# Forgetting attention with its query blocks in the order last, third, first, second, two of them in one group

## The reference

```
proj = hn @ fox_w_in[j]
qc, kc, vc, fz = split(proj)
log_f = log_sigmoid(fz + fox_b_f[j])
c = cumsum(log_f)                                   # per head, over the tokens
# per block of 128 queries:
logits = (q_block @ k^T) * HEAD_DIM ** -0.5 + c[query] - c[key]
logits = where(key <= query, logits, -inf)
out    = softmax(logits) @ v
mixed  = out @ fox_w_out[j]
```

## Time and profile before

| | |
|---|---|
| median of 3 runs | 2126.46 us (2125.49 to 2126.67) |
| span of the profiled execution | 2125.2 us |
| mean granted TensorE clock | 0.998 |
| TensorE busy | 2088.4 us (98%) |
| VectorE, ScalarE, GpSimd busy | 1435.0, 852.2, 748.9 us |
| the forgetting attention's iterations 1 to 8 | from about 1470 to 1669 us of the span |

### The profile page before, as it was taken

One profiled execution on the slowest core, in us unless ns is written; L12 is line 12 of the kernel. 1 busy time (PEld: TensorE's weight loads), 2 busy tenths in 40 slices (PEclk: granted clock), 3 DMA queues, 4 the chain that ended last, 5 costly groups with the idle time before them and its releaser, 6 DMA issues.

```text
span 2125.2 us, 37888 instructions
## 1 busy us (share of the span) xinstructions
PE 2088.4 (98%) x15232; PEld 1808.2 (85%) x15232; DVE 1435.0 (68%) x1748; ACT 852.2 (40%) x1154; POOL 748.9 (35%) x646
## 2 busy tenths in 40 slices
PE   8999999999989999999999999999999999999998
PEld 6989898778887899999788898987776689998977
DVE  7847576679757866666778575766666677575774
ACT  6434243454233433333444243434444344343434
POOL 2333244546433214243443151433333322423343
PEclk9999999999999999999999999999999999999999
DMA  5333332321012334243342332424223232433332
GB/s 160 90 109 103 97 86 85 97 60 41 14 33 61 101 91 119 79 117 88 100 123 77 107 105 86 119 70 120 79 79 95 74 99 80 120 90 106 89 93 90
DMA packets 366507, 192.95 MB, mean 91 GB/s; under 512 B 11038, under 2 KB 363408, under 8 KB 366368
## 3 DMA queue, kind: packets, MB, share of 16 engines
q1 hardware_dynamic: 364128, 185.11, 31.0%
q0 software_dynamic: 2224, 5.86, 0.9%
q10 hardware_dynamic: 16, 0.00, 0.0%
HBM read 188.81 MB, written 2.13 MB: 90 GB/s over the span
## 4 chain that ended last, share of the span: by engine, by line
PE 89%; DVE 7%; ACT 2%; issue 1%; DMA 0%; ACTq 0%; POOL 0%; DVEq 0%; SPq 0%; POOLq 0%
PE bank L468 13%; PE bank L470 13%; PE bank L469 13%; PE bank L633 11%; PE bank L634 11%; PE bank L635 11%; PE bank L1914 3%; PE bank L2575 2%; DVE w_lo L458 2%; PE bank L2577 2%; PE bank L2576 2%; PE bank L1255 1%; PE bank L1257 1%; PE bank L1256 1%; PE bank L2592 1%
## 5 line engine op out<-in xcount | busy, mean ns | idle before, releaser
L458 DVE TENSOR_TENSOR w_lo<-w_raw,w_hi 128x2048 fp32r<-128x2048 f32 (+3 forms) x192 | 393.4, 2049 | 137.6 <-ACT w_hi L453 136.6
L453 ACT CAST w_hi<-w_raw 128x2048 fp32r<-128x2048 f32 (+3 forms) x192 | 281.6, 1467 | 387.2 <-PE bank L635 169.7
L619 POOL TENSOR_TENSOR sums<-w_raw 128x512 f32<-128x512 f32 x68 | 95.8, 1409 | 778.0 <-DMA w_raw<-in_ffn_w_gu_dram 520.4
L468 PE MATMUL bank<-h_hi,w_hi 128*128 128x512 f32 x704 | 275.4, 391 | 1.8 <-DVE w_lo L458 1.5
L469 PE MATMUL bank<-h_hi,w_lo 128*128 128x512 f32 x704 | 274.2, 389 | 0.0
L470 PE MATMUL bank<-h_lo,w_hi 128*128 128x512 f32 x704 | 274.1, 389 | 0.0
L975 DVE SCALAR_TENSOR_TENSOR x<-bank,x 128x512 f32<-128x512 f32 (+1 forms) x96 | 66.4, 691 | 166.5 <-PE bank L470 165.5
L468 PEld LDWEIGHTS bank<-h_hi,w_hi 128*128 128x128 f32 x704 | 132.1, 188 | 34.8 <-issue 4.8
L633 PE MATMUL bank<-t_hi,s_hi 128*128 128x256 f32 x544 | 154.4, 284 | 1.7 <-issue 1.7
L470 PEld LDWEIGHTS bank<-h_lo,w_hi 128*128 128x128 f32 x704 | 132.1, 188 | 27.6
L469 PEld LDWEIGHTS bank<-h_hi,w_lo 128*128 128x128 f32 x704 | 132.2, 188 | 26.2
(11 more groups left out here) (390 smaller groups left out, 5444.5 us busy)
## 6 DMA issues: line engine op xcount, KB each, us to landing
w_raw<-in_ffn_w_gu_dram SPq DMA_DIRECT2D x176, 512.0 KB, 5.0
w_raw<-in_ffn_w_down_dram SPq DMA_DIRECT2D x128, 256.0 KB, 3.1
w_raw<-in_ffn_w_down_dram SPq DMA_DIRECT2D x64, 192.0 KB, 3.1
w_raw<-in_even_w_in_dram SPq DMA_DIRECT2D x40, 256.0 KB, 3.2
w_raw<-in_ple_w_gate_dram SPq DMA_DIRECT2D x16, 512.0 KB, 3.7
w_raw<-in_fox_w_in_dram SPq DMA_DIRECT2D x16, 512.0 KB, 5.0
w_raw<-in_even_w_out_dram SPq DMA_DIRECT2D x16, 256.0 KB, 3.4
w_raw<-in_fox_w_in_dram SPq DMA_DIRECT2D x16, 256.0 KB, 4.1
```

Source lines behind the costliest of these rows:

```text
L453: nc.scalar.copy(w_hi[slot][:, 0:tiles], w_raw[slot][:, 0:tiles]).then_inc(w_hi_ready, 1)
L458: nc.vector.tensor_tensor(w_lo[slot][:, 0:tiles], w_raw[slot][:, 0:tiles], w_hi[slot][:, 0:tiles].bitcast(F32), ALU.subtract).then_inc(w_r ...
L468: nc.tensor.matmul(dst, w[0], hi[:, k], start=k == 0, stop=False)
L619: nc.gpsimd.tensor_tensor(sums[:, 0:4], w[:, 8:12], w[:, 12:16], ALU.add).then_inc(sums_made, 1)
```

## The change

The units of a pair come in another order of query blocks, and two of them are handled together on TensorE. `FOX_ORDER = (3, 2, 0, 1)`: unit 0 is still the last block (512 columns) and unit 1 the third (384), but unit 2 is now the first block (128 columns) and unit 3 the second (256). 384 and 128 columns fill one bank of 512, so unit 2 is placed from column 384 on (`unit_place`) in the same banks as unit 1, for the products as for the transposes.

`logits(1, 2)` makes the products of both units one behind the other after a single wait, and signals `qk_done` once, by 2, at the end. `transposes(1, 2)` does the same for the transposes. `transposes` signals `pt_ready` in every case only once, at its end, where it signalled behind each head before. There is thus one run of weight groups fewer to interrupt: the products come ahead of weight groups 0, 5 and 9 (before: 0, 5, 8 and 10), the transposes ahead of groups 12, 16 and 20 (before: 12, 15, 18 and 21). The orders of the other engines stay as they were, unit by unit; only the block that a unit stands for and its columns in the bank differ.

The core of the diff:

```
+FOX_ORDER = (3, 2, 0, 1)
...
-            qb = NB - 1 - u
+            qb = FOX_ORDER[u]
             return qb * (qb + 1) // 2 * P, (qb + 1) * P
+
+        def unit_place(u):
+
+            return (NB - 1) * P if u == 2 else 0
...
-                def logits(u):
+                def logits(*units):
                     if not attend:
                         return
-                    if u == 0:
+                    if units[0] == 0:
                         pe.wait_ge(banks_free, n - 1)
                         pe.wait_ge(logit_ready, a * (2 * NB)) if not isinstance(a, int) or a else None
                     else:
-                        pe.wait_ge(logit_ready, a * (2 * NB) + 2 * u)
...
+                        pe.wait_ge(logit_ready, a * (2 * NB) + 2 * units[0])
+                    for u in units:
+                        qb = FOX_ORDER[u]
+                        for h in range(2):
+                            rows = slice(h * HD, (h + 1) * HD)
+                            mm = nc.tensor.matmul(bank[4 + h][:, unit_place(u):unit_place(u) + (qb + 1) * P],
+                                                  fox_q[rows, qb * P:(qb + 1) * P],
+                                                  fox_k[rows, 0:(qb + 1) * P], start=True, stop=True)
+                    mm.then_inc(qk_done, len(units))
...
+                def transposes(*units):
...
-                    for h in range(2):
-                        pe.wait_ge(p_ready, a * (2 * NB) + (2 * u + h + 1))
-                        for kb in range(qb + 1):
-                            mm = nc.tensor.transpose(bank[6 + h][:, kb * P:(kb + 1) * P],
-                                                     fox_logit[:, h, at + kb * P:at + (kb + 1) * P],
-                                                     ident[:])
-                        mm.then_inc(pt_ready, 1)
+                        pe.wait_ge(pt_copied, a * (2 * NB) + 2 * units[0])
+                    for u in units:
+                        qb = FOX_ORDER[u]
+                        at, _ = unit_cols(u)
+                        for h in range(2):
+                            pe.wait_ge(p_ready, a * (2 * NB) + (2 * u + h + 1))
+                            for kb in range(qb + 1):
+                                to = unit_place(u) + kb * P
+                                mm = nc.tensor.transpose(bank[6 + h][:, to:to + P],
+                                                         fox_logit[:, h, at + kb * P:at + (kb + 1) * P],
+                                                         ident[:])
+                    mm.then_inc(pt_ready, 2 * len(units))
...
-                logits(1)
-                groups(5, 8)
-                logits(2)
-                groups(8, 10)
+                logits(1, 2)
+                groups(5, 9)
                 logits(3)
-                groups(10, 12)
+                groups(9, 12)
                 transposes(0)
-                groups(12, 15)
-                transposes(1)
-                groups(15, 18)
-                transposes(2)
-                groups(18, 21)
+                groups(12, 16)
+                transposes(1, 2)
+                groups(16, 20)
                 transposes(3)
-                groups(21, 24)
+                groups(20, 24)
```

More of the change, by code:

```diff
@@ L2587, in logits @@
                     else:
-                        pe.wait_ge(logit_ready, a * (2 * NB) + 2 * u)
-                    qb = NB - 1 - u
-                    for h in range(2):
[L2591 to L2597, removed]
+                        pe.wait_ge(logit_ready, a * (2 * NB) + 2 * units[0])
[8 more added lines that the diff above has]
+                def transposes(*units):
                     if not attend:
                         return
-                    qb = NB - 1 - u
-                    at, _ = unit_cols(u)
-                    if u == 0:
+                    if units[0] == 0:
                         pe.wait_ge(vt_copied, a + 1)
@@ L2606, in transposes @@
                     else:
-                        pe.wait_ge(pt_copied, a * (2 * NB) + 2 * u)
-                    for h in range(2):
-                        pe.wait_ge(p_ready, a * (2 * NB) + (2 * u + h + 1))
-                        for kb in range(qb + 1):
-                            mm = nc.tensor.transpose(bank[6 + h][:, kb * P:(kb + 1) * P],
-                                                     fox_logit[:, h, at + kb * P:at + (kb + 1) * P],
-                                                     ident[:])
-                        mm.then_inc(pt_ready, 1)
+                        pe.wait_ge(pt_copied, a * (2 * NB) + 2 * units[0])
[10 more added lines that the diff above has]
+                    mm.then_inc(pt_ready, 2 * len(units))
                 def times_values():
@@ L2725, in copy_pt @@
                         nc.scalar.copy(fox_pt[:, h, 0:qb + 1, qb * P:(qb + 1) * P],
-                                       bank[6 + h][:, 0:(qb + 1) * P].rearrange("p (k q) -> p k q", q=P)
+                                       bank[6 + h][:, unit_place(u):unit_place(u) + (qb + 1) * P].rearrange("p (k q) -> p k q", q=P)
                                        ).then_inc(pt_copied, 1)
@@ L2802, in logits @@
                         return
-                    qb = NB - 1 - u
+                    qb = FOX_ORDER[u]
                     at, cols = unit_cols(u)
+                    place = unit_place(u)
                     dve.wait_ge(qk_done, a * NB + (u + 1))
@@ L2811, in logits @@
                             nc.vector.scalar_tensor_tensor(
-                                fox_logit[:, h, at:at + qb * P], bank[4 + h][:, 0:qb * P], cq[h],
+                                fox_logit[:, h, at:at + qb * P], bank[4 + h][:, place:place + qb * P], cq[h],
                                 fox_c[:, h, 0:qb * P], ALU.add, ALU.subtract)
                         nc.vector.scalar_tensor_tensor(
-                            fox_logit[:, h, at + qb * P:at + cols], bank[4 + h][:, qb * P:cols], cq[h],
+                            fox_logit[:, h, at + qb * P:at + cols], bank[4 + h][:, place + qb * P:place + cols], cq[h],
                             fox_cm[:, h, qb], ALU.add, ALU.subtract).then_inc(logit_ready, 1)
@@ L2898, in pair @@
                             fox_logit[:, h, at:at + cols], fox_logit[:, h, at:at + cols],
-                            fox_rcp[:, NB - 1 - u, h:h + 1].broadcast_to([P, cols]), ALU.mult
+                            fox_rcp[:, FOX_ORDER[u], h:h + 1].broadcast_to([P, cols]), ALU.mult
                         ).then_inc(p_ready, 1)
```

## The result

The changed kernel takes 2132.81 us (median of 8 runs, 2132.15 to 2135.31), the kernel before 2126.43 beside it: a ratio of 1.0029 with a 95% interval of 1.0021 to 1.0038, +6.4 us. A later series gave 2133.22 against 2126.18, 1.0033 (1.0021 to 1.0045). The changed kernel is slower by 0.3%.

The account below looks back on a forecast made before the run. TensorE's own stream was taken to set the pace (25.50 us busy of 25.50). Merged products -3.2, products' wait +6.0, transposes' wait +3.3, end of iteration 8 +0.3: +6.4 on 2126.46, 2132.9 us; range 2129.0 to 2135.0.

Parts of the forecast that it names:

- rival A: The forecast itself: both new waits of TensorE appear, 2131.3 to 2134.5 us by the bounds of the terms; chance 0.72.
- merged products, per pair: TensorE's merged logit group pays its width-independent part once: 0.40 us saved per pair, -3.2 us over eight pairs.
- merged transposes, per pair: TensorE's merged transposes have no fixed part to save: 0, with bounds of +-0.05 us per pair.
- bank free after the merged products' start: VectorE has taken units 1 and 2 out of the shared bank 4.86 us after the start; TensorE comes at 4.03.
- wait ahead of the last products, net iteration: TensorE stands still until VectorE frees the bank: seven times 0.83 us and once 0.2, +6.0 us.
- last transposes after the merged ones' start: ScalarE's copies of units 1 and 2, rounding between them, allow the last transposes at 4.18 us; TensorE comes at 3.63.
- transposes' wait, net iteration: TensorE waits 0.55 us for ScalarE's copies ahead of the last transposes in iterations 1 to 6: +3.3 us.
- the fixed part: Part of each logit group's time on TensorE that does not depend on its width: 0.40 us, paid once when merged.
- The edges: Iteration 1: products' wait only 0.2 us; iteration 7: no transposes' wait; end of iteration 8: +0.3 us.
- the rival of half the gain: Unit 2's weight loads in the merged products do not overlap matmuls: 1.6 us more, 2134.5 us; chance 0.04.
- the prediction's estimate: At about 26 ns per increment, 6 instead of 12 signalling instructions per pair would save 1.2 us over eight pairs; not counted.

Follow-up runs that it names:

- products merged and cured: Changed kernel with transposes separate and signalling per head, last products ahead of weight group 10, y_lo behind unit 2's logits: 2122.96 us, ratio 0.9986.
- rounding first: Changed kernel with last products ahead of weight group 11 and ScalarE rounding the next weights ahead of the copies of units 1 and 2: 2123.78 us, ratio 0.9989.
- products alone merged: Changed kernel, but transposes separate at their old places with a signal per head; new order and merged products kept: 2128.81 us, ratio 1.0010.
- both cures: Changed kernel with last products ahead of weight group 11, not 9, and ScalarE's copies of unit 2 ahead of the weight rounding: 2126.88 us, ratio 1.0000.
- the last products later alone: Changed kernel, but with the last products ahead of weight group 11 instead of 9: 2128.24 us, ratio 1.0004.

## Why the prediction was right

**The time** came out at +6.4 us as forecast, and the steady iteration at 26.50 as forecast. That the time agrees to the tenth is luck: the later series gave +7.0, and the stage by itself is 6.0 longer (below). The bounds of the terms, added up, give 2130.7 to 2134.7 and not the 2131.3 to 2134.5 that stand at rival A; the result lies in both. Term by term, from the profiles (predicted, then measured):

| term | predicted | measured | from |
|---|---|---|---|
| merged products, per pair | -0.40 | -0.44 | 25.06 against 25.50, products merged and cured |
| merged transposes, per pair | 0 | -0.03 | 25.03 against 25.06, rounding first |
| bank free after the merged products' start | 4.86 | 4.84 | products alone merged, changed kernel |
| wait ahead of the last products, net iteration | 0.83 | 0.81 | 25.87 less 25.06 |
| last transposes after the merged ones' start | 4.18 | 4.21 | changed kernel |
| transposes' wait, net iteration | 0.55 | 0.60 | 26.10 less 25.50 |

**The bottleneck** was read rightly: each hole of TensorE in this stage went into the time, and the one-edit kernels add up, -0.44 + 0.81 + 0.60 = 0.97 against 0.99 to 1.00 measured together. So neither wait follows from the other: each is there without the other in the kernels with the products or the transposes alone merged.

**The merged products** saved slightly more than the fixed part. The x8 group is busy 1.14 us, where the forecast said about 1.1 and bare loads of unit 2 would have made it 1.3. Its weight loads in the changed kernel:

```profile
1551.74 0.95 PEld L2598 LDWEIGHTS bank<-fox_k,fox_q 64*128 64x128 f32 x8 [0.35 <-issue]
```

All eight loads are through 0.95 us after the group began; a single one lasts 0.18 to 0.19 us, so the last began at about 0.77, while unit 1's matmuls, 0.92 us by themselves, still ran. With that the rival of half the gain falls. The Trainium skill's sentence behind it ("TensorE: Matmul & The Clock Gate", Part 3, the mechanism), that a load overlaps a running matmul only when the row groups differ, does not hold by itself for this form; the measurement decides. The merged transposes, which take five signals away (six signalling instructions per pair in *The rounding first*, eleven in *The products merged and cured*), bring the iteration 0.03 us at most. The same page's tail of about 26 ns per increment (Part 3, per-tile semaphore tail), taken as a price for every signal as the prediction's estimate takes it, would have asked for 0.13; the runs do not bear that use of it out.

**The edges were mis-sized**, each a little: iteration 1 +0.2 (0.35 forecast), iteration 7 +0.3 (0.43), iteration 8 up to the last products with the values +0.55 (0.73). In iteration 7 VectorE starts 1.19 us after the merged group, not 1.30, so the wait is 0.1 shorter. From its first products to the last products with the values the stage takes 202.66 and 202.64 us in the two profiles of the changed kernel and 196.62 before: 6.0 us longer, not 6.4.

**The rest up to 6.4** is not settled run by run. The first profile of the changed kernel ended iteration 8 so, TensorE's last transposes and the last products with the values, and the windows around them:

```profile
1666.82 1.04 PE L2619 MATMUL bank<-ident,fox_logit 128*128 128x128 f32 x8
1669.15 0.66 PE L2619 MATMUL bank<-ident,fox_logit 128*128 128x128 f32 x4 [1.29 <-ACT fox_pt L2729]
1670.54 4.07 PE L2683 MATMUL bank<-fox_pt,fox_vt 128*64 128x512 f32 x16 [0.73 <-ACT fox_pt L2729]
```

```profile
1667.00:1670.50 3.50, 1.52 (x12) 1.04 (x10) 0.00 (x0) 1.85 (x6) 0.00 (x0) 1.00 0.00 0
1670.50:1674.70 4.20, 4.07 (x16) 1.56 (x16) 0.00 (x0) 0.05 (x1) 0.00 (x0) 0.59 0.00 0
```

The last products with the values took 4.07 us instead of the 2.38 of the earlier trace rows, at a granted clock of 0.59 over that stretch, that is, mostly at the lower of the two levels, 1.2 GHz; ahead of it TensorE was busy for 1.52 of 3.50 us. In the second profile of the same kernel they follow the same holes at the full clock:

```profile
1671.30 0.66 PE L2619 MATMUL bank<-ident,fox_logit 128*128 128x128 f32 x4 [1.29 <-ACT fox_pt L2729]
1672.69 2.38 PE L2683 MATMUL bank<-fox_pt,fox_vt 128*64 128x512 f32 x16 [0.73 <-ACT fox_pt L2729]
```

So the fall comes and goes from execution to execution. Of the thirteen profiles of this study it is in six, the one with the order alone among them, which has no new wait, and in neither of the two fastest. The prediction had not counted on it; the last products with the values take 3.64 to 4.54 us when it comes, so it is worth 1.3 to 2.2 us. Whether the longer holes behind merged transposes make it come more often is open: five of the nine profiles with merged transposes have it and one of the four without, too few to tell.

## What to carry to other kernels

Before merging two small steps on the engine that sets the pace, walk the other engines' paths from the merged step's one signal to the next thing that this engine waits for, and compare with the work left between them: here 4.86 against 4.03 us and 4.18 against 3.63, differences that the timelines of the kernel before gave to 0.05 us. A merge that takes away an interruption also takes away a run of work that was a cover, so the order around it, on all engines, has to be laid out anew; done so, the merge of the products was worth 3.2 us, and that of products and transposes together 2.4, where the change as it stood cost 6.4. And what one cure delays is the next wait: look for it in the following iteration, not only behind the edit.

## What the runs showed of the hardware

VectorE's w_lo for 16 tiles (128 x 2048, two inputs in SBUF) lasts between 2.29 and 4.50 us in the iterations of this stage in the thirteen profiles, and what decides is whether, and by how much, GpSimd's fox_cm begins ahead of it. With both cures GpSimd's fox_cm begins first, ends in its 2.39 us, and w_lo takes 4.35 (rows in *Both cures*). With the last products later alone it is the other way round, VectorE and then GpSimd in one iteration:

```profile
1540.01 2.29 DVE L459 TENSOR_TENSOR w_lo<-w_raw,w_hi 128x2048 fp32r<-128x2048 f32 x1 [2.28 <-ACT w_hi L454]
```

```profile
1540.20 4.34 POOL L2895 TENSOR_TENSOR fox_cm<-fox_c,causal 128x1024 f32<-128x1024 f32 x1 [3.57 <-DMA fox_c<-cum_dram]
```

w_lo starts 0.19 us ahead, takes 2.29, and fox_cm stretches to 4.34. That is what the Trainium skill states in "SBUF — State Buffer", "Who interferes with whom": a VectorE instruction with two SBUF inputs contends with a GpSimd one that reads SBUF, and the order of issue decides which one blocks. These runs agree. Whoever reads the kernel before alone would take w_lo's 3.97 us for its own length; 1.7 of it (3.97 less 2.29) was waiting for fox_cm.
